# Delta stage of a two-layer decoder step: channel blocks projected over 512 prompt tokens, sample tokens projected once per weight block and transposed

## What is computed

```python
def _deltanet_mixer(h, s0, buf, w_in, conv_w, a_log, dt_bias, norm_g, w_out):
    p = h @ w_in                                    # 1024 -> 4096 (q, k, v) + 2048 (z) + 32 (a, b)
    qkv, buf_new = _causal_conv(p[..., :DN_CONV_CH], buf, conv_w)      # width 4, channel by channel
    qkv = jax.nn.silu(qkv).astype(F32)
    z = p[..., DN_CONV_CH:DN_CONV_CH + DN_VW]
    ...
    o, s = _gated_delta_chunked(q, k, v, g, beta, s0.astype(F32))      # chunks, triangular solve, state
    o = _rms_norm(o, norm_g) * jax.nn.silu(z...)
    return o.reshape(B, L, DN_VW).astype(h.dtype) @ w_out, s, buf_new
```

## Time and profile before

| | us |
|---|---|
| median of 3 runs | 2220.41 (2220.36 to 2223.27) |
| profiled execution, its own time | 2225.8 |
| its span in the profile | 2224.0 |
| PE busy in the span | 1867.9 (84%) |
| segment 0 of the delta stage | 1033.05 to 1110.57 |
| segment 1 | 1110.57 to 1285.33 |
| segment 2 | 1285.33 to 1458.74 |
| segment 3 | 1458.74 to 1635.64 |
| segment 4 | from 1635.64 |

### The profile page before, as it was taken

The page is one execution under the profiler, slowest core; times in us unless marked ns, Lnnn a source line. Parts: engine busy times, 40 slices in busy tenths (PEclk is TensorE's granted clock), DMA queues, the critical chain, the costliest instruction groups (busy, mean ns, idle before and its releaser), DMA issues. The chain is left out here.

```text
span 2224.0 us, 35412 instructions
## 1 busy us (share of the span) xinstructions
PE 1867.9 (84%) x14911; PEld 983.7 (44%) x14911; DVE 794.3 (36%) x1644; ACT 384.2 (17%) x847; POOL 359.7 (16%) x458
## 2 busy tenths in 40 slices
PE   4999999999899859956998998998996869939970
PEld 3443443434234433325756755755754634423320
DVE  0122333233332330015445546646545424240108
ACT  1010000110000012113432232332231100002211
POOL 0020110101102300022431031031121002120104
PEclk9999999999879879977998998998996889959985
DMA  9355738556260199978233033133124583068964
GB/s 342 138 206 196 257 103 296 183 181 215 93 216 38 41 368 398 399 272 269 97 104 108 13 102 87 51 100 87 47 70 138 196 237 117 19 251 300 402 247 151
DMA packets 232299, 396.66 MB, mean 178 GB/s; under 512 B 16909, under 2 KB 88213, under 8 KB 232086
## 3 DMA queue, kind: packets, MB, share of 16 engines
q1 hardware_dynamic: 226190, 372.90, 47.8%
q0 software_dynamic: 5952, 21.50, 2.5%
HBM read 300.86 MB, written 93.51 MB: 177 GB/s over the span
## 5 line engine op out<-in xcount | busy, mean ns | idle before, releaser
L552 PE MATMUL bank<-ring,hT 128*128 128x512 f32 x768 | 343.7, 598 | 3.3 <-PEq L267 2.2
L1162 PE MATMUL bank<-hT,ring 128*128 128x272 f32 x1024 | 293.7, 424 | 5.0 <-PEq L2493 5.0
L552 PEld LDWEIGHTS bank<-ring,hT 128*128 128x128 f32 x768 | 141.7, 190 | 187.5 <-issue 184.8
L1162 PEld LDWEIGHTS bank<-hT,ring 128*128 128x128 f32 x1024 | 191.7, 200 | 56.5 <-issue 22.1
L2284 PE MATMUL bank<-expert_w,exp_xT 128*32 128x512 f32 x1152 | 176.1, 618 | 15.8 <-DMA expert_w<-in_moe_w_gu_dram 11.8
L2877 PE MATMUL bank<-ring,oT 128*128 128x512 f32 x384 | 175.1, 618 | 13.6 <-DMA oT<-oT_spill 13.0
L2877 PEld LDWEIGHTS bank<-ring,oT 128*128 128x128 f32 x384 | 75.6, 198 | 108.3 <-issue 95.1
L1159 PE MATMUL bank<-ring,hT 128*128 128x512 f32 x256 | 115.4, 596 | 0.0
L2284 PEld LDWEIGHTS bank<-expert_w,exp_xT 128*32 128x32 f32 x1152 | 47.4, 113 | 125.4 <-issue 120.2
L2308 PE MATMUL bank<-expert_w,exp_aT 128*32 128x512 f32 x576 | 88.5, 605 | 10.8 <-DMA expert_w<-in_moe_w_down_dram 9.4
L2378 DVE TENSOR_TENSOR exp_a<-bank,exp_sg 128x256 f32<-128x256 f32 x24 | 10.2, 425 | 222.0 <-ACT exp_sg L2361 222.0
(11 more groups left out here) (449 smaller groups left out, 2563.8 us busy)
## 6 DMA issues: line engine op xcount, KB each, us to landing
ring<-in_w_ada_dram SPq DMA_DIRECT2D x24, 2048.0 KB, 9.1
expert_w<-in_moe_w_gu_dram SPq DMA_DIRECT2D x24, 2048.0 KB, 17.5
expert_outputs<-ret_zeros SPq DMA_DIRECT2D x15, 2048.0 KB, 10.1
expert_w<-in_moe_w_down_dram SPq DMA_DIRECT2D x24, 1024.0 KB, 16.6
ring<-in_ret_w_in_dram SPq DMA_DIRECT2D x8, 2048.0 KB, 13.8
ret_Ss<-in_state_ret_dram SPq DMA_DIRECT2D x32, 512.0 KB, 5.4
out_dram<-ret_Ss SPq DMA_DIRECT2D x32, 512.0 KB, 3.1
oT<-in_moe_w_gu_dram SPq DMA_DIRECT2D x8, 2048.0 KB
```

The costliest lines, as they stand in the source:

```text
L552: last = pe.matmul(ps[u % 2][:, :], core.hT[:, k, tok(t)], core.ring[:, w % RING, k, :], start=(k == 0), stop=(k == KD - 1))
L1162: mm = pe.matmul(ps[U % 2][:, 0:HALF], core.ring[:, w % RING, k, c * P:(c + 1) * P], core.hT[:, k, half * HALF:(half + 1) * HALF], start=( ...
```

## The change

A channel block becomes one unit: eight matmuls of 512 prompt columns. The sample tokens leave the channel blocks. Ahead of the four channel blocks of each b=0 and b=1 block stands a sample unit (c = -1). It multiplies the 32 sample tokens by the whole weight block, in the form that z's fifth unit has: 32 matmuls of 128 columns in four column groups, all issued at item k = 7. ACT copies the 128x128 result out (`smp_rows`), PE transposes it in a new step ST placed after item k = 3 of the next unit, ACT copies it out again (`smpT`), and each channel block takes its 32 columns from there. A group has 15 units instead of 21, and the places of the gate steps are written anew.

```diff
-                n = NT * (j + 1) if l == 0 else 21 * (j // 3) + (8, 16, 21)[j % 3]
+                n = NT * (j + 1) if l == 0 else 15 * (j // 3) + (5, 10, 15)[j % 3]
...
-    UN = 21
-    HALF = NTOK // 2
+    UN = 15
...
-        GBs, Ems, Els = (st.sb(n, [P, G, NS]) for n in ("GBs", "Ems", "Els"))
+        Ems, Els = (st.sb(n, [P, G, NS]) for n in ("Ems", "Els"))
+        smp_rows, smpT = core.res, st.sb("smpT", [P, P])
+        GBs = flat(kd)[:, 0:G * NS].rearrange("p (g n) -> p g n", n=NS)
...
-        GATE = {KD - 1: [("GA", 0)], 2 * KD: [("GB", 0)], 4 * KD: [("GC", 0)], 5 * KD: [("GD", 0)], 7 * KD: [("GE", 0)],
-                8 * KD: [("GF", 0)], 9 * KD: [("GG", 0)], 12 * KD: [("GH", 0)]}
-        for t_ in range(NT):
-            GATE[(2 * t_ + 3) * KD + 4] = [("GX", t_)]
+        GATE = {(1, 2): [("GA", 0)], (1, 5): [("GB", 0)], (2, 2): [("GC", 0)], (2, 5): [("GD", 0)], (3, 2): [("GE", 0)],
+                (3, 5): [("GF", 0)], (4, 2): [("GG", 0)], (6, 2): [("GH", 0)], (9, 0): [("GY", 0)]}
+        for n, U in enumerate((2, 3, 4, 6, 7)):
+            GATE[(U, 0)] = [("GX", n)]
...
-            first = [0] + [UN * g + 16 for g in range(G)] + [UN * G]
+            first = [0] + [UN * g + 10 for g in range(G)] + [UN * G]
             for g in range(G + 1):
-                mm = [("mm", U, k) for U in range(first[g], first[g + 1]) for k in range(KD)]
+                mm = []
+                for U in range(first[g], first[g + 1]):
+                    for k in range(KD):
+                        mm.append(("mm", U, k))
+                        if k == 3 and U and samples(U - 1):
+                            mm.append(("ST", *unit(U - 1)[0:2]))
...
-            return s["pre_parts"], 4 * fc(g, b, c) + 2 + 2 * half
+            if c < 0:
+                return s["smpT_kept"], 2 * g + b + 1
+            return s["pre_parts"], 3 * fc(g, b, c) + 2
...
-                    if b == 2 and c == NPT:
+                    if samples(U) or (b == 2 and c == NPT):
...
-                        mm = pe.matmul(ps[U % 2][:, 0:HALF], core.ring[:, w % RING, k, c * P:(c + 1) * P],
-                                       core.hT[:, k, half * HALF:(half + 1) * HALF], start=(k == 0), stop=(k == KD - 1))
+                        mm = pe.matmul(ps[U % 2][:, :], core.ring[:, w % RING, k, c * P:(c + 1) * P],
+                                       core.hT[:, k, 0:SEQ], start=(k == 0), stop=(k == KD - 1))
...
+                def turn_samples(g, b):
+                    pe.wait_ge(s["smp_rows"], 2 * g + b + 1)
+                    pe.transpose(ps[(UN * g + 5 * b) % 2][:, P:2 * P], smp_rows[:], ident[:, :]).then_inc(s["st_ps"], 1)
...
+                    if samples(U):
+                        if g or b:
+                            act.wait_ge(s["st_ps"], 2 * g + b)
+                        act.activation(smp_rows[:], ps[U % 2][:, 0:P], ACT.Copy).then_inc(s["smp_rows"], 1)
+                        return
...
+                    act.activation(pre[:, r, 3:3 + SEQ], ps[U % 2][:, :], ACT.Copy).then_inc(s["pre_parts"], 1)
+                    act.wait_ge(s["smpT_kept"], 2 * g + b + 1)
+                    act.activation(seqs[:, :, 3:7], smpT[:, NS * c:NS * (c + 1)].rearrange("p (b w) -> p b w", w=DECL),
                                    ACT.Copy).then_inc(s["pre_parts"], 1)
+                def turned_samples(g, b):
+                    act.wait_ge(s["st_ps"], 2 * g + b + 1)
+                    act.activation(smpT[:], ps[(UN * g + 5 * b) % 2][:, P:2 * P], ACT.Copy).then_inc(s["smpT_kept"], 1)
```

More of the change, by code:

```diff
@@ L999, in unit, with samples @@
             g, r = U // UN, U % UN
-            if r < 16:
-                return g, r // 8, (r % 8) // 2, r % 2
-            return g, 2, r - 16, 0
+            if r < 10:
+                return g, r // 5, r % 5 - 1
+            return g, 2, r - 10
+        def samples(U):
+            g, b, c = unit(U)
+            return b < 2 and c < 0
         def fc(g, b, c):
@@ L1010, in taken @@
         def taken(U):
-            g, b, c, half = unit(U)
+            g, b, c = unit(U)
             if b == 2:
                 return s["z_taken"], NT * g + c + 1
-            return s["pre_parts"], 4 * fc(g, b, c) + 2 + 2 * half
+            if c < 0:
+                return s["smpT_kept"], 2 * g + b + 1
+            return s["pre_parts"], 3 * fc(g, b, c) + 2
         res = pre[:].rearrange("p r n -> p (r n)")[:, 0:8 * P].rearrange("p (i c) -> p i c", c=P)
@@ L1065, in _ @@
                 state_in(0)
-                first = {UN * g + u: 3 * g + j for g in range(G) for j, u in enumerate((0, 8, 16))}
+                first = {UN * g + u: 3 * g + j for g in range(G) for j, u in enumerate((0, 5, 10))}
                 def step(what, x, h):
@@ L1081, in step @@
                         decay_in(1)
-                    if what == "GH":
+                    if what == "GY":
                         for n in range(NT):
@@ L1445, in _ @@
                         continue
+                    if what == "ST":
+                        turn_samples(x, l)
                     gate_step(what)
@@ L1652, in step @@
                 def step(what, x, l):
+                    if what == "ST":
+                        turned_samples(x, l)
                     gate_step(what)
@@ L1686, in project, with convolved @@
                             pool.tensor_tensor(zs[:, :], zs[:, :], ng[:, :], ALU.mult).then_inc(s["zg_done"], 1)
-                    elif half == 1:
+                def convolved(U):
+                    g, b, c = unit(U)
+                    if b < 2 and c >= 0:
                         F, ch = fc(g, b, c), channel(g, b, c)
@@ L1744, in step @@
                         pool.tensor_tensor(rsn[:], ssn[:], core.eps[:, 3:4], ALU.pow).then_inc(s["rsn_done"], 1)
-                follow(project, step)
+                follow(project, step, convolved, KD - 1)
             @block.vector
@@ L1793, in convolve @@
                 def convolve(U):
-                    g, b, c, half = unit(U)
-                    if b == 2 or half == 0:
+                    g, b, c = unit(U)
+                    if b == 2 or c < 0:
                         return
                     F, ch = fc(g, b, c), channel(g, b, c)
-                    dve.wait_ge(s["pre_parts"], 4 * F + 4)
+                    dve.wait_ge(s["pre_parts"], 3 * F + 3)
                     if F:
```

25 lines of the change are left out of this document (10 added, 15 removed).

## The result

The changed kernel takes 2277.01 us (median of 4, 2273.62 to 2280.12) against 2221.84 us: 1.0245 times, 95% interval 1.0225 to 1.0265. The forecast was 2263 us and slower.

What follows compares the result with a forecast made beforehand. PE was taken to pace the stage, with idle waits for the recurrence, mostly DVE. 1.9 - 2.6 + 19.4 + 17.8 + 6.3 = +42.8 us took 2225.8 to 2268.6, less 5.4 for the median: 2263 us, range 2224 to 2286.

Steps and rivals of the forecast that it cites:

- The work of the new form: PE's matmuls: channel blocks save 14.4 us, sample units add 14.9 and transposes 1.4; sum +1.9 us.
- Segment 0: Gate steps move, so PE's 2.59 us wait for DVE at GE goes: -2.6 us, bounds 0 and +4.1.
- Empty places: Segments 1 to 3: z's fifth and first sample unit leave recurrence steps without projection-matmul cover: +19.4 us.
- Order on DVE: Segments 1 to 3: convolution moves ahead of the second half's S3, wait 3.63 to 6.6 us; net +6.3 us.
- The second sample unit: The b=1 block's unit leaves C3, X, P, CV and X uncovered, with a convolution at k = 3: +3.0 us a segment.
- The 3.9 us that denser matmuls were to fill: Half of segment 1's other 7.7 us of idle time taken as filled by denser channel matmuls: -3.9 us a segment.
- The clock: Segments 1 to 3: half rate behind the uncovered waits slows PE's matmuls: +17.8 us, bounds 0 and about +32.
- ST: Rival: ACT's list holds back the copy ST waits for, +18 us on top, 2281 us; chance 0.13.
- paid back: Rival: PE's work stays the bound and denser matmuls fill existing waits, about 2203 us, faster; chance 0.08.
- The milder case (clock soon back): Rival: only the uncovered waits cost, clock kept or soon back, +19 to +25 us, about 2243 us; chance 0.22.
- The signs named beforehand: Segments 1 to 3 each 12 to 18 us longer, PE idle 22 to 25 us, PEclk about 0.90.

Runs made afterwards that it cites:

- Run 1: Kernel before, matmuls unchanged, with empty items in its written list so recurrence steps fall as in the changed kernel: 2285.53 us, 1.0274.
- run 3: Changed kernel with each narrow unit issuing four of its 32 matmuls at each of its eight items: 2263.55 us, 1.0173.
- run 2: Changed kernel with projection items in segments 1 to 3 placed by their time instead of by count: 2280.28 us, 1.0257.
- run 4: Changed kernel with 63 added matmuls of 384 columns, results unread, at the empty items of segments 1 to 3: 2268.60 us, 1.0189.
- run 5: Changed kernel with DVE's convolution issued as four passes at k = 3, 4, 5 and 6: 2264.66 us, 1.0165.
- run 6: Changed kernel with items placed by their time and the convolution in four pieces: 2249.09 us, 1.0108.
- run 12: Changed kernel with convolution at k = 1, 63 added 384-column matmuls at empty items, three added ahead of the second half's S3: 2264.70 us, 1.0176.
- run 8: Changed kernel with narrow matmuls spread four per item, items placed by time and the convolution in four pieces: 2249.76 us, 1.0111.
- run 9: Changed kernel with the convolution in one piece at item k = 1 instead of k = 3: 2275.43 us, 1.0241.
- version 10: Changed kernel with narrow matmuls spread four per item, items placed by time and the convolution in one piece at k = 4: 2245.39 us, 1.0085.
- run 7: Kernel before with DVE's convolution in four pieces: 2246.32 us, 1.0103.
- run 11: Kernel before with three added 512-column matmuls, results unread, ahead of the second half's S3 in segments 1 to 3: 2234.56 us, 1.0042.

## Why the prediction was right

*The work of the new form.* Taken as +1.9 us, 0.864 us a matmul; 0.858 measured. Run 1 has the loss without it. Right, with one reading to mend: the 0.16 us for a change of form were taken from the earlier trace rows, where both rows have 128x128 weights and no form changes. In the kernel before, at full clock, two records of line 1159 take 0.86 us up to a step with 128x128 weights (1659.48 to 1660.34) and 0.95 up to one with 32x32 weights (1660.78 to 1661.73), and run 3 has 0.14 us for a stretch. The 1.86 us of the earlier trace rows hold the change already, so the sum needs no further term for it.

*Segment 0.* -2.6 us for a wait at GE that would go. It did not: 2.75 us instead of 2.59. The segment is 1.2 us shorter all the same. The term was wrong, and small. What decides it is a collision. DVE's and POOL's timelines ahead of that wait:

```profile
1053.04 2.35 POOL L1704 TENSOR_TENSOR dn_va<-dn_va,dn_A 128x1024 f32<-128x1024 f32 x1 [21.30 <-DMA dn_ng<-in_dn_norm_g_dram]
1053.19 2.30 DVE L1800 TENSOR_TENSOR dn_Rv<-dn_Rv 128x80 f32<-128x80 f32 x1
1055.46 2.34 POOL L1705 TENSOR_TENSOR dn_va<-dn_va,dn_A 128x1024 f32<-128x1024 f32 x1
1055.52 2.38 DVE L1801 SCALAR_TENSOR_TENSOR dn_g<-dn_Rv 128x80 f32<-128x80 f32 x1
```

The same in run 2, whose segment 0 is the same code:

```profile
1054.35 0.24 DVE L1811 TENSOR_TENSOR dn_Rv<-dn_Rv 128x80 f32<-128x80 f32 x1
1054.63 0.24 DVE L1812 SCALAR_TENSOR_TENSOR dn_g<-dn_Rv 128x80 f32<-128x80 f32 x1
1055.45 2.35 POOL L1715 TENSOR_TENSOR dn_va<-dn_va,dn_A 128x1024 f32<-128x1024 f32 x1 [21.82 <-DMA dn_ng<-in_dn_norm_g_dram]
```

Two DVE operations of 0.24 us last 2.3 us each when POOL's operation runs beside them, and PE's wait is 2.75 us; when POOL starts after them, PE has no idle time at all in segment 0, which is then 71.08 us long instead of 76.35 (2.75 us of the difference are the wait, 2.5 PE's busy time). Runs 3, 4, 5, 6 and 12 have one or two such long operations, runs 8, 9 and 10 none. So in some executions the wait went as forecast, and in the profiled one it did not.

*Empty places.* The term was read off segment 4: 9.7 us of waits in each segment. In segment 1 they are 3.18 + 4.28 = 7.5 us, in segment 2 8.6 (3.52, 1.11 and 3.96), in segment 3 7.5 (3.19 and 4.28). The place and the mechanism are right. In segments 1 and 3 they are 2 us less than forecast, the first being 3.2 instead of 4.9 and the last one gone; in segment 2, where less was forecast (7.8 us), they are 0.8 us more. One wait that grew was not foreseen, at S1 of the second half: 4.18 us in segment 1 and 1.84 in segment 3, where the kernel before has 1.23 and 1.27. The trace puts it down to issue. SP's list shows the store of the state and then its load, issued from 1159.68 to 1166.95 in segment 1. In all runs, wherever S1 waits 0.9 us or more, it starts 4.2 to 5.7 us after the last load was issued, and in segment 4, where the trace mostly names the transfer for the same wait, 4.9 to 5.7. So it waits for the transfer. PE comes 0.6 or 0.7 us earlier after the store than it did before, and in segment 1 the transfer also takes 2.2 us longer. No run moved the transfer alone.

*Order on DVE.* 3.63 was to become 6.6 us; 6.59, 5.74 and 6.59 were measured. The second sample unit was taken at +3.0 us and has 0.53 + 1.96 + 1.67 = 4.2 us of waits in segment 1, 3.4 in segment 2 and 3.6 in segment 3. The 3.9 us that denser matmuls were to fill came short: at C5 the waits are 0.92, 1.44 and 3.09 us. All of it together, with what stood at these steps before taken off:

| waits of PE in segments 1 to 3, us | forecast | measured |
|---|---|---|
| empty places: first X, second S3 | +19.4 | +16.3 |
| S1 of the second half | 0 | +3.2 |
| S3 of the second half, convolution in front | +9.0 | +8.2 |
| stretch of the second sample unit | +9.0 | +11.2 |
| all other waits | -11.7 | -6.9 |
| sum | +25.7 | +32.0 |

The fourth line holds a wait of another kind, which the forecast did not have. Of the 11.2 us, 3.7 (1.67, 0.95 and 1.12) fall in the middle of a step X, between its 47th and its 48th record in segment 1 (1231.42 and 1233.85 above), where no step waits for another engine. The trace calls it issue. Its DMA view shows the 2 MB transfer of a weight block holding all 16 DMA engines up to 1231.0, and then one packet of the instruction queue; PE goes on 2.4 to 2.9 us after that packet. Segment 2 of this kernel, run 1 (3.58 us in segment 1), run 4 (2.46), run 5 (4.07) and segment 4 of the kernel before (3.85) show the same: PE goes on 2.2 to 2.9 us after such a packet. So in stretches of many short matmuls PE probably runs out of instructions while weights are being loaded. It was not tested by a run, and in runs 1 and 5, with 10 us in three segments each, it is a part of the loss that neither cover nor DVE's order explains.

*The clock.* +17.8 us with the work's +1.9 were foreseen; measured are 18.3 us of busy time more in segments 1 to 3, and 1.6 of the 2.5 us in segment 4, in its first z stretch. That these agree so well is partly luck, since what the sum is made of was partly mistaken: the second sample unit too ran at half clock (3.64 us in each segment), and so did a part of the first z stretch of segment 2, 16.33 us instead of 14.76, behind a last wait of 3.09 us; the forecast had leaned on 2.93 us doing no harm. Runs 4 and 12 show the clock's share: with work added, the rest of PE's work took 13 and 25 us less.

*Sum.* +42.8 us foreseen, +47.8 in the profiled execution, +55.2 between the medians. The last 7 us come from which executions were profiled: the changed kernel's is the fastest of its runs, 3.4 us below their median, and that of the kernel before is 4.0 us above its median.

*Rivals.* Ahead of its eight transposes ST has 0.5 us of idle time in all. The wait at S3 grew, so nothing was paid back. The milder case (clock soon back) fell with PEclk at 0.88 to 0.90.

*The signs named beforehand.* Segments 1 to 3 were to be 12 to 18 us longer each and are 16.3, 20.2 and 13.8. PE's idle time was to be 22 to 25 us and is 25.8 to 28.7: too low, by the waits of the table. The clock and the place of the longest waits were as foreseen.

What stays open: why version 10 still needs 1% more than the kernel before. In its profiled execution segments 1 to 3 take 24 us more, 12 of them waits, and differ by up to 17 us among each other. The record shows these candidates: the wait at S1 for the state's transfer (2.76, 3.95 and 3.62 us), the convolution ahead of a C5 in segment 2 (4.74 us), the 0.14 us for each stretch of narrow matmuls, and waits for instructions (1.44 us in segment 3). No run separates them.

## What to carry to other kernels

When a list is written by count of items, an item without work is a hole, and a dependent step that falls in it has nothing to cover its wait. This can be priced before building: another stretch of the same trace, where these steps already stand uncovered, gave the single waits to within 2 us.

A change of the unit's size moves more than matmuls. It moved one 3.0 us operation of another engine from before a step to behind it. Moving or cutting that operation alone was worth between -1.5% (run 6 against 2) and +1.0% (run 7), and once nothing, because the wait went elsewhere (run 9). Write out what each engine has in front of the step that the bound engine waits for, in both orders.

## What was not expected of the hardware

Adding 41 us of TensorE work in the gaps made the kernel no slower (run 4), and 49 us made it faster than its twin without it (run 12 against 9).

An operation of 0.24 us on DVE lasted 2.3 us beside one of POOL that took 2.35 (account of segment 0, above).

Waits of one and the same length stood ahead of either clock. In run 11 PE waits 2.92 us for C5 at the end of segment 1 and again at the end of segment 2 (PE's timeline of run 11):

```profile
1292.45 0.66 PE L1290 MATMUL bank<-ident,dn_ob 128*128 128x128 f32 x4 [2.92 <-DVE dn_ob L1897]
...
1461.48 1.12 PE L1290 MATMUL bank<-ident,dn_ob 128*128 128x128 f32 x4 [2.92 <-DVE dn_ob L1897]
```

The same four transposes take 0.66 us behind the one and 1.12 us behind the other. In the changed kernel the z matmuls behind C5 waits of 3.09, 3.08 and 3.09 us take 16.33, 15.11 and 16.40 us for the 34 records that take 14.76 at full clock. In run 2 a C5 behind a wait of 3.54 us takes 0.66 us in segments 1 and 3 and 1.12 in segment 2. The Trainium skill, TensorE: Matmul & The Clock Gate, section What's actually happening, says that the measurement behind the clock runs on freely, so that the moment of a change depends on where the activity falls in it; these rows agree with it. For a forecast it means that a wait near 3 us has no fixed price.
